# The MLP's first 512 features: from two plain blocks to one turn with a seven-product down projection

## The reference

```python
z = rmsnorm(h, norm_mlp)                                # 1024 x 1024
h = h + jnp.square(jax.nn.relu(z @ w_up)) @ w_down      # w_up 1024 x 4096, w_down 4096 x 1024
return rmsnorm(h, norm_final)
```

## Time and profile before

| | before |
|---|---|
| median of 3 runs | 1489.59 us |
| lowest and highest | 1489.36 and 1492.01 us |
| the profiled execution, its time | 1491.61 us |
| its span in the trace | 1489.6 us |
| TensorE busy in the span | 1466.8 us (98%) |
| VectorE, ScalarE, GpSimd busy | 971.7, 518.9, 519.7 us |
| the MLP's first matmul after the output projection | at 846.64 us |
| first matmul of the seven turns | at 935.81 us |

### The profile page before, as it was taken

One profiled execution on the slowest core, in us unless ns is written; L12 is line 12 of the kernel. 1 busy time (PEld: TensorE's weight loads), 2 busy tenths in 40 slices (PEclk: granted clock), 3 DMA queues, 4 the chain that ended last, 5 costly groups with the idle time before them and its releaser, 6 DMA issues.

```text
span 1489.6 us, 20639 instructions
## 1 busy us (share of the span) xinstructions
PE 1466.8 (98%) x7019; PEld 1210.4 (81%) x7019; DVE 971.7 (65%) x1911; ACT 518.9 (35%) x1003; POOL 519.7 (35%) x349
## 2 busy tenths in 40 slices
PE   9999999999999999999999999999999999999995
PEld 8887888888888888888888888888888888888884
DVE  6898665552367627676623797685857676767678
ACT  7422322300122212241101332544445444445455
POOL 4000001246333242003433002373737464646556
PEclk9999999999999999999999999999999999999998
DMA  7224534273211111013552001333333333333333
GB/s 222 96 93 137 143 103 128 81 254 107 63 45 43 31 42 57 15 43 113 184 191 71 1 29 50 101 105 113 108 111 102 109 113 107 111 111 107 113 110 137
DMA packets 150934, 149.04 MB, mean 100 GB/s; under 512 B 19104, under 2 KB 109904, under 8 KB 150864
## 3 DMA queue, kind: packets, MB, share of 16 engines
q1 hardware_dynamic: 118048, 107.00, 23.1%
q10 hardware_dynamic: 32816, 41.12, 8.5%
HBM read 126.58 MB, written 21.50 MB: 99 GB/s over the span
## 4 chain that ended last, share of the span: by engine, by line
PE 91%; DVE 5%; ACT 1%; issue 1%; ACTq 1%; DMA 0%; POOL 0%; DVEq 0%
PE acc L817 20%; PE acc L819 20%; PE acc L818 20%; PE aux L817 9%; PE aux L818 8%; PE aux L819 8%; PE aux L1099 1%; PE aux L1092 1%; PE aux L1102 1%; PE aux L982 1%; PE aux L976 0%; PE aux L1087 0%; PE aux L1108 0%; PE aux L1182 0%; DVE w_lo L2064 0%
## 5 line engine op out<-in xcount | busy, mean ns | idle before, releaser
L817 PE MATMUL acc<-z_hi,w_hi 128*128 128x512 f32 x448 | 177.2, 396 | 0.6 <-DVE z_lo L1893 0.6
L819 PE MATMUL acc<-z_hi,w_lo 128*128 128x512 f32 x448 | 174.6, 390 | 0.0
L818 PE MATMUL acc<-z_lo,w_hi 128*128 128x512 f32 x448 | 174.5, 390 | 0.0
L817 PE MATMUL acc<-w_hi,z_hi 128*128 128x512 f32 x384 | 164.4, 428 | 0.0
L819 PE MATMUL acc<-w_hi,z_lo 128*128 128x512 f32 x384 | 150.5, 392 | 0.0
L818 PE MATMUL acc<-w_lo,z_hi 128*128 128x512 f32 x384 | 149.6, 390 | 0.0
L677 POOL CAST w_hi<-stage 128x1024 fp32r<-128x1024 f32 x22 | 28.0, 1271 | 346.1 <-PE acc L819 291.7
L664 POOL TENSOR_SCALAR stage<-stage,nm 128x512 f32<-128x512 f32 x48 | 78.4, 1644 | 168.9 <-PE acc L819 87.3
L785 POOL TENSOR_TENSOR t_raw<-t_raw,p_a 128x512 f32<-128x512 f32 x28 | 38.5, 1375 | 248.7 <-DMA p_a<-in_w_up 155.8
L817 PEld LDWEIGHTS acc<-z_hi,w_hi 128*128 128x128 f32 x448 | 84.1, 188 | 19.9 <-issue 1.5
L819 PEld LDWEIGHTS acc<-z_hi,w_lo 128*128 128x128 f32 x448 | 84.1, 188 | 17.8
(11 more groups left out here) (417 smaller groups left out, 3871.6 us busy)
## 6 DMA issues: line engine op xcount, KB each, us to landing
stage<-in_w_in SPq DMA_DIRECT2D x28, 512.0 KB, 4.9
p_a<-in_w_up SPq DMA_DIRECT2D x56, 256.0 KB, 2.8
p_a<-in_w_down SPq DMA_DIRECT2D x56, 256.0 KB, 2.7
gate_dram<-gate_t ACTq DMA_DIRECT2D x32, 256.0 KB, 2.1
p_b<-in_w_up SPq DMA_DIRECT2D x28, 256.0 KB, 2.7
p_b<-in_w_down SPq DMA_DIRECT2D x28, 256.0 KB, 2.6
x_in<-in_x SPq DMA_DIRECT2D x8, 512.0 KB, 6.5
stage<-in_w_in SPq DMA_DIRECT2D x32, 128.0 KB, 2.3
```

The costliest lines, as they stand in the source:

```text
L817: nc.tensor.matmul(out, s_hi, m_hi_, start=first, stop=False, skip_group_check=partial)
L818: nc.tensor.matmul(out, s_hi, m_lo_, start=False, stop=False, skip_group_check=partial)
L819: return nc.tensor.matmul(out, s_lo, m_hi_, start=False, stop=last, skip_group_check=partial)
```

## The change

The two plain blocks are replaced by one turn, also of 512 features, so that the MLP is eight turns. Its up projection stays plain: `first_block(0)` and `first_block(1)` on TensorE, 8 tiles of 24 matmuls. Its weights are eight pieces of the ring's size (`first_piece`), loaded by SyncE (`load_first`), cast by ScalarE (`first_hi`), subtracted by GpSimd (`first_lo`). First piece 6 shares slot 3 with first piece 3 and is loaded once the first four tiles (0 to 3) are finished; it is used by tile 5. Its down projection is the seven-product form of the other turns: `down_block(0, False, True)`, 14 steps of 12 matmuls. The hidden tiles go to `hid_raw` (`first_square` on ScalarE: relu, then square). The down pieces 14 to 20 are loaded during the up projection, as `first_used` and `out_ready` free the slots, in the order 14, 15, 16, (first piece 6), 18, 19, 17, 20. The sums of z are formed in a row at the head of VectorE's part, `lo_s1` in steps 21 and 23 of the down projection, and the low parts of `s4_sum` behind the last `add_pair`. The buffers and semaphores of the plain blocks are gone.

```diff
-            for f in range(N_PLAIN):
-                plain_block(f)
-            win_block(0, True)
-            with pe.Fori(1, N_WIN - 1) as g:
+            pe.wait_ge(lo_done, SP_Z2 + 8)
+            first_block(0)
+            first_block(1)
+            down_block(0, False, True)
+            win_block(1, True)
+            with pe.Fori(2, N_WIN - 1) as g:
                 win_block(g, False)
             win_block(N_WIN - 1, last=True)
...
+            def first_block(s):
                 for half in range(2):
                     for q in range(FT):
-                        n = n0 + FT * half + q
-                        if f == 0 and n == OUT_MLP + 1:
+                        n = 4 * s + 2 * half + q
+                        if n == 1:
                             turn_z2(NCH - 2)
-                        if f == 0 and half == 1 and q == 0:
+                        if n == 2:
                             pe.wait_ge(lo_done, SP_Z2 + 16)
...
+                        for kh in range(2):
+                            i = 4 * s + 2 * q + kh
+                            if half == 0:
+                                pe.wait_ge(first_ready, FIRST_ORDER.index(i) + 1)
+                            hi, lo = [w.rearrange("p (k c) -> p k c", k=KH) for w in first_piece(i)[:2]]
+                            for k in range(KH):
...
+                            if half == 1 and kh == 0:
+                                mm.then_inc(first_used, 1)
                         mm.then_inc(out_ready, 1)
...
+                if 3 <= c < 7:
+                    first_hi(c - 3)
...
+                if first:
+                    for n in (4, 5, 7):
+                        first_hi(FIRST_ORDER.index(n))
+                    for n in range(4):
+                        first_square(n)
+                    first_hi(7)
+                    hidden_hi(0)
+                    cast_pieces(UP_PIECES - 4, 0, least=UP_PIECES)
+                    first_square(4)
+                    hidden_hi(1)
+                    cast_s(s2_hi, s2_sum, (3, 4))
+                    first_square(5)
+                    cast_s(s3_hi, s3_sum, (6, 6))
+                    cast_pieces(UP_PIECES - 3, 0, least=UP_PIECES)
+                    cast_pieces(UP_PIECES - 2, 0, least=UP_PIECES)
+                    first_square(6)
+                    first_square(7)
+                    hidden_hi(2)
+                    cast_pieces(UP_PIECES - 1, 0, least=UP_PIECES)
...
+                if first:
+                    for u in range(2):
+                        form_s1(u)
+                    for u in range(2):
+                        form_s2(u)
+                    for u in range(2):
+                        form_s3(u)
+                    hidden_lo(0)
+                    hidden_s3(0)
+                    hidden_s1(0)
+                    hidden_s2(0)
+                    piece_lo(14)
+                    hidden_lo(1)
...
+                    if first and s in (21, 23):
+                        lo_s1((s - 21) // 2)
```

## The result

| | before | after |
|---|---|---|
| median (22 runs each) | 1489.97 us | 1492.29 us |
| lowest and highest | 1489.21, 1492.01 | 1490.24, 1495.05 |
| the profiled execution, its time and span | 1491.61, 1489.6 | 1495.05, 1493.3 |
| from the MLP's start (below) to the end of the span | 649.29 | 651.91 |

The ratio of after to before is 1.0018, with a 95% interval of 1.0011 to 1.0024: 2.3 us slower by the medians. 1493.3 was forecast, within a range of 1487.0 to 1496.5.

A forecast was written before the change was run, and what follows sets the result against it. TensorE, busy 98%, was taken to bound the kernel, with VectorE nearly late. Terms -5.44 + 0.25 + 6.35 + 0.35 (a turn's remaining usual loss) + 2.0 + 0.2 = +3.7 gave 1493.3 us, range 1487.0 to 1496.5.

The forecast's parts named there:

- -5.44 for 24 matmuls: New turn's down projection on TensorE: 168 matmuls instead of 192, 0.2267 us each, 5.44 us less.
- First piece 6, +0.25: Up projection, tile 5: the piece's late slot, load, cast and GpSimd subtraction delay TensorE by 0.25 us (0 to 1.2).
- VectorE's queue, +6.35: New down projection, steps 2, 3 and 5: VectorE's work plus GpSimd's holds make TensorE 6.35 us late.
- restarts: TensorE's slower rows after a wait, 0.47 and 0.50 instead of 0.39: +0.2 us.
- the term of 0.55 for each subtraction beside a chunk's scaling: Head: GpSimd's four subtractions for pieces 0 to 3 hold VectorE's chunk scaling 0.55 us each, +2.2 in all.
- Holds at 1.2 each: VectorE's queue up to step 2: six GpSimd subtractions and sums cost it 1.2 us each, 7.2 in all.
- The tail, +2.0: Two `lo_s1` low parts at steps 21 and 23 make VectorE late, with a wait at step 12: +2.0 us (1.0 to 2.8).
- The clock rival: Waits at steps 2 and 3 drop TensorE's clock, a dozen or so slower matmuls cost +2.5: 1496 us; chance 0.06.
- VectorE isn't held: Rival: GpSimd yields, the 7.2 and 2.2 us vanish, piece 17 decides: 1488.4 us (1486.6 to 1490.5); chance 0.23.
- all is hidden: Rival: other engines' work stays hidden as in the plain blocks, but for a turn's usual 0.5: 1484.7 us; chance 0.09.

The follow-up runs named there:

- e_s4_tail: e_s4_order plus v_tail's edit (low parts of s1 behind the last add_pair, s4's casts and low parts inside turn 1); s4_sum holds other values: 1484.42 us.
- v_slot2: Changed kernel with first piece 6 in slot 2 instead of 3, piece 17 loaded in its old place and piece 16 last: 1491.73 us.
- v_tail: Changed kernel with the two low parts of s1 behind the last add_pair, s4's casts and low parts inside turn 1: 1491.49 us.
- e_gps_none: Changed kernel without GpSimd's subtractions for first pieces 4 to 7; ScalarE writes plain copies, so numbers aren't the reference's: 1489.18 us.
- v_more: v_all with the low parts of pieces 18 and 19 of every turn on VectorE instead of GpSimd: 1494.09 us.
- v_all: Changed kernel with v_tail's edit, first piece 6 in slot 2, VectorE subtracting first pieces 4 to 7, earlier casts of first pieces 0 to 3: 1487.86 us.
- after_again: The changed kernel once more, nothing altered: 1492.70 us.
- e_s4_order: e_s4_slot2 with ScalarE's order mended: piece 15's cast ahead of hidden tile 4's square, s2's casts and the two copies behind it: 1488.21 us.
- e_s4_slot2: Changed kernel with form_s4 on VectorE replaced by two ScalarE copies (s4_sum holds other values) and first piece 6 in slot 2: 1491.37 us.

## Why the prediction was right

- **-5.44 for 24 matmuls**: right. With every wait gone, 5.07 came through (e_s4_tail).
- **First piece 6, +0.25**: 0.30 in the timeline, 0.43 by v_slot2. Right in place; the row names no releaser, but GpSimd's subtraction ends 0.05 ahead of it.
- **VectorE's queue, +6.35**: right in mechanism, 1.1 too large: the trace has 5.29, that is 5.16 and the 0.13 of a usual turn, and restarts, for which the sum had another 0.2, are in it. The laid-out queue itself, 35.0 of work and 7.2 of holds, was 42.2; from 858.67 to 900.87 the trace shows 42.2. What was mis-sized, by 0.9, is its start. I had it 34.0 ahead of the down projection, and it began 893.56 - 858.67 = 34.9 ahead. Of that, the larger part is the term of 0.55 for each subtraction beside a chunk's scaling: `zb` took 1.66 instead of 1.28, so 0.38 (four times 0.17 = 0.7 less). I had chosen the middle between 0 and 1.25 with no row for it. Hidden tile 2 was ready at +7.3 instead of +8.2, and step 2 waited 1.85 instead of 2.8.
- **Holds at 1.2 each**: 1.0 each in the `form_s` rows, and seven of them instead of six (the trace has first piece 4's too). That the two errors cancel is luck.
- **The tail, +2.0**: 2.08, and v_tail shows that the two low parts are its cause. The wait at step 12 came (0.35), with two more at steps 10 and 13.
- **The clock rival** (0.06, 1496): half right. The clock fell in the profiled execution, behind a wait of 1.85, shorter than the 2.8 that I had forecast. But the 2.5 that I added for it were wrong: in this kernel a slower TensorE in front of a late VectorE loses nothing (71.06 with the fall, 71.04 without).
- **"VectorE isn't held"** (0.23) and **"all is hidden"** (0.09): refuted by the rows of 2.2 and by the waits. Their numbers were sound: 1484.7 for "all is hidden" against 1484.42 for e_s4_tail, and piece 17 as the next cause, which e_gps_none brought up.
- The sum was +3.7 and the trace has +2.6; the medians moved by 2.3, from 1489.97.

## What to carry to other kernels

Lay out the queue of the engine that is nearly late, instruction by instruction, and add what a neighbour's instructions hold it for; here that came out to a tenth of a us over 42. Count from a mark behind which executions repeat, and judge a section by its whole length, since single waits move between steps. Before you give work to another engine, ask what stands beside it: here a subtraction of GpSimd costs VectorE 1.0 beside an instruction on SBUF and nothing beside an add from PSUM. And ask what moves up into the place of what you take away: in v_more other GpSimd instructions did, and the holds stayed.

## What the runs showed of the hardware

- In the rows read here GpSimd and VectorE took turns, whole instructions at a time, where both had their inputs in SBUF. A full VectorE queue lost 1.0 for each instruction of GpSimd (1.22 to 2.20), and GpSimd's own took 2.27 instead of 1.29. The Trainium skill, SBUF — State Buffer, "Who interferes with whom", says that these two exclude each other; the rows agree.
- The granted clock fell to half behind a wait of 1.85 (after) and of 1.83 (v_all), and did not behind those of 1.79 and 2.09 in the same program (after_again). In the new turn of all traces waits of 1.79 to 2.09 ended with a fall seven times and without one five times. It stayed at 1.00 in the one trace where float32 matmuls of 64 rows filled all but 0.39 of the gap. The Trainium skill, TensorE: Matmul & The Clock Gate, Part 1, has an idle array go back to half rate. The traces agree that idleness brings it, and show that waits of nearly the same length can end either way.
- A fall made six to nine matmuls take 0.43 instead of 0.2267. It cost nothing where a later wait for VectorE took that up (after and after_again), and 0.8 us where too little of one was left (behind step 12 in e_s4_order and e_s4_slot2).
